# Inverting the chunk matrices of a delta-rule recurrence on TensorE: where the transposed inverse of each level comes from

## What is computed

```
def step(state, inp):
    r_t, w_t, k_t, v_t, kk_t, a_t = inp
    sa = jnp.einsum('bhvk,bhk->bhv', state, kk_t)
    state = (state * w_t[:, :, None, :]
             - sa[..., None] * (kk_t * a_t)[:, :, None, :]
             + v_t[..., None] * k_t[:, :, None, :])
    return state, jnp.einsum('bhvk,bhk->bhv', state, r_t)
```

## Time and profile before

| | |
|---|---|
| median of 3 runs | 3971.02 us (3969.14 to 3973.49) |
| span of the profiled execution | 3972.0 us |
| TensorE busy, of the whole span | 3709.6 us, 93% |
| VectorE busy | 2670.4 us, 67% |
| GpSimd busy | 1955.5 us, 49% |
| the eight tiles' levels and what lies between them | from 515 to 990 us |

### The profile page before, as it was taken

How to read it: one execution, slowest core, us unless ns; L and a number is a source line. 1 busy time by engine, 2 the same in 40 slices (tenths; PEclk the granted TensorE clock), 3 DMA queues, 4 the chain that set the end, 5 groups by cost and what they waited for, 6 DMA issues and landing times.

```text
span 3972.0 us, 55158 instructions
## 1 busy us (share of the span) xinstructions
PE 3709.6 (93%) x19324; PEld 3187.3 (80%) x19324; DVE 2670.4 (67%) x5202; ACT 1244.6 (31%) x1825; POOL 1955.5 (49%) x1352
## 2 busy tenths in 40 slices
PE   8988799999898899999999999999789999899999
PEld 6854488988777678899999998999667888678777
DVE  5443367776322438748887887877797666598887
ACT  3013333332211321233333333323233333333333
POOL 1023122222100016888888888888888888222220
PEclk9989989999999999999999999999889999999999
DMA  3259400000320034478888888887889999899997
GB/s 114 95 192 399 163 19 9 18 18 0 106 90 27 27 106 92 78 199 264 265 270 269 265 261 247 260 263 212 246 210 278 278 282 253 282 384 381 371 380 267
DMA packets 376223, 788.61 MB, mean 199 GB/s; under 512 B 136992, under 2 KB 245536, under 8 KB 342176
## 3 DMA queue, kind: packets, MB, share of 16 engines
q1 hardware_dynamic: 210208, 451.28, 33.7%
q0 software_dynamic: 165888, 336.01, 28.9%
HBM read 643.09 MB, written 144.05 MB: 198 GB/s over the span
## 4 chain that ended last, share of the span: by engine, by line
PE 26%; POOL 15%; DMA 7%; DVE 6%; issue 6%; DVEq 2%; ACT 1%; SPq 1%; POOLq 0%; ACTq 0%
POOL gates_d L2066 12%; PE peer_ps L2176 12%; PE peer_ps L2085 9%; PE peer_ps L2099 4%; DMA peer_gat<-gates_d 3%; DMA late_in<-gates_d 3%; POOL rows L2054 2%; POOL peer_rows L2054 2%; DVE late_rows L2459 1%; DVEq L2389 1%; DVE peer_acc L2474 1%; PE peer_ps L2122 1%; DVEq L2473 1%; DVE late_in L2481 1%; DVE peer_al L2493 0%
## 5 line engine op out<-in xcount | busy, mean ns | idle before, releaser
L2066 POOL DMA_INDIRECT gates_d<-peer_gates,peer_idx x768 | 1366.5, 1779 | 300.9 <-issue 221.2
L2085 PE MATMUL peer_ps<-high,peer_uh 128*128 128x384 f32 x2048 | 528.8, 339 | 38.0 <-DVE peer_ul L2376 32.0
L2085 PE MATMUL peer_ps<-low,peer_uh 128*128 128x384 f32 x2048 | 524.2, 337 | 0.0
L2085 PE MATMUL peer_ps<-high,peer_ul 128*128 128x384 f32 x2048 | 523.6, 336 | 0.0
L2085 PEld LDWEIGHTS peer_ps<-high,peer_uh 128*128 128x128 f32 x2048 | 370.5, 189 | 51.5 <-issue 44.5
L2085 PEld LDWEIGHTS peer_ps<-low,peer_uh 128*128 128x128 f32 x2048 | 373.7, 190 | 0.0
L2085 PEld LDWEIGHTS peer_ps<-high,peer_ul 128*128 128x128 f32 x2048 | 373.3, 189 | 0.0
L2176 PE MATMUL peer_ps<-peer_vh,peer_ah 128*128 128x512 f32 x1026 | 326.8, 400 | 40.3 <-DVE peer_al L2493 40.0
L2054 POOL DMA_INDIRECT late_rows<-in_expert_uv,peer_idx x108 | 139.1, 1288 | 412.1 <-DVE peer_acc L2474 369.6
L2176 PE MATMUL peer_ps<-peer_vh,peer_al 128*128 128x512 f32 x1026 | 322.1, 395 | 0.0
L2176 PE MATMUL peer_ps<-peer_vl,peer_ah 128*128 128x512 f32 x1026 | 321.4, 395 | 0.0
(11 more groups left out here) (480 smaller groups left out, 7697.4 us busy)
## 6 DMA issues: line engine op xcount, KB each, us to landing
late_in<-in_expert_uv SPq DMA_DIRECT2D x170, 512.0 KB
gates_d<-mla_zeros POOLq DMA_DIRECT2D x128, 512.0 KB
hidden_d<-peer_hid SPq DMA_DIRECT2D x128, 384.0 KB
peer_raw<-in_expert_u SPq DMA_DIRECT2D x86, 512.0 KB
peer_val<-in_expert_uv SPq DMA_DIRECT2D x86, 512.0 KB
late_in<-hidden_d SPq DMA_DIRECT2D x170, 192.0 KB
late_in<-gates_d SPq DMA_DIRECT2D x170, 192.0 KB
first_raw<-in_expert_u SPq DMA_DIRECT2D x42, 512.0 KB
```

Of the source, the lines that this page charges most:

```text
L2066: pool.indirect_dma_start(gates_flat, bass.IndirectOffsetOnAxis(ap=idx[:, n, k:k + 1], axis=0), gates[:, n, k:k + 1], None, compute_op=ALU ...
L2085: last = nc.tensor.matmul(ps[i][:, a, 0:HD], w[:, cols], x[:, kc, a * HD:(a + 1) * HD], start=(kc == 0 and w is uh[i % 2] and x is high), ...
```

## The change

At levels 1 to 4 the third product (z transposed) and the masked copy into `yi[e]` go. Instead TensorE transposes the new X itself, `xi[e]`, into `bank[4 + e]`, directly after the next level's P products of that half, and signals a new semaphore `x_turned`. VectorE, after both masked copies into `xi`, waits for it and copies the whole bank into `yi[e]`. The preparing step of the level on VectorE stays behind these copies.

```
@@ TensorE, solve, level l, half e @@
                         inc(last, "p_mm")
+                        if l > 1:
+                            for f in range(PAIRS):
+                                last = nc.tensor.transpose(bank[4 + e][:, f, :], xi[e][:, f, :], consts["ident"][:, :])
+                            inc(last, "x_turned")
...
                         for f in range(PAIRS):
                             last = nc.tensor.matmul(bank[2 + e][:, f, :], yi[e][:, f, :], pe_s[e][:, f, :],
                                                     start=True, stop=True)
-                            if l < 5:
-                                last = nc.tensor.matmul(bank[4 + e][:, f, :], pe_s[e][:, f, :], yi[e][:, f, :],
-                                                        start=True, stop=True)
                         inc(last, "z_mm")
@@ VectorE, solve, level l @@
                         inc(nc.vector.copy_predicated(xi[e][:, :, :], where(level_t, l), bank[2 + e][:, :, :]), "inv")
-                        if l < 5:
-                            inc(nc.vector.copy_predicated(yi[e][:, :, :], where(consts["level"], l),
-                                                          bank[4 + e][:, :, :]), "inv_t")
+                    if l < 5:
+                        for e in range(2):
+                            w.wait("x_turned", 2 * (l - 1) + e + 1)
+                            inc(nc.vector.tensor_copy(flat(yi[e]), flat(bank[4 + e])), "inv_t")
                     if l > 1:
                         prepare_next(l - 1)
```

More of the change, by code:

```diff
@@ L875, in rwkv_stage @@
                         ("ux", 1), ("ux_taken", 1), ("preset", 2), ("copied", 2), ("inv", 12), ("inv_t", 10), ("p_mm", 10), ("p_taken", 10),
-                        ("z_mm", 10), ("u_mm", 2), ("nu", 2), ("at_mm", 2), ("e_mm", 2), ("diag", 2), ("at", 2),
+                        ("z_mm", 10), ("x_turned", 8), ("u_mm", 2), ("nu", 2), ("at_mm", 2), ("e_mm", 2), ("diag", 2), ("at", 2),
                         ("q_mm", 1), ("q1", 1), ("chain", 2), ("state", 2), ("y_mm", 1), ("y", 1), ("mean", 1),
```

## The result

The changed kernel takes 3977.41 us, the median of 20 runs (3967.26 to 4014.81); the kernel before took 3962.26 us beside it (20 runs, 3945.06 to 3979.01). The ratio is 1.0046, 95% interval 1.0031 to 1.0061: slower by about 18 us (the medians themselves lie 15.2 us apart).

What follows compares the result with a forecast made beforehand. TensorE was taken to end levels 2 and 3 of a loop tile, VectorE levels 1 and 4. Queues +12.5 and clock +10.5 gave +23 us on 3972.0, 3995; 1 us less for the median: 3994 us, range 3975 to 4013.

Steps and rivals of the forecast that it cites:

- rival 1: Recurrence: queues cost time but TensorE's pauses pass without a clock fall; +12.5 us, 3983.5 us; chance 0.25.
- The queue on VectorE: Loop tiles: preparing work waits behind `yi` copies; steps 4.77, 8.1 to 8.2, 8.61, 5.37 us; +2.3 us a tile.
- Leaving level 5: End of a tile's levels: second `xi` copy and `kap` come sooner, 1.34 instead of 1.74 us, -0.40 us.
- The prices: Levels 1 to 4: four transposes take 0.44 us, a copy from PSUM into `yi` 0.69 us.
- The dear end of this term: Levels 1 to 4: transposes as slow as products, 0.90 for 0.44 us, add +6.0 us a tile.
- The clock: First seven tiles: TensorE's pauses bring one fall each to 0.50 for 3.4 us, costing 1.5 us; 10.5 us total.
- I leave both as they are: Recurrence: the two clock falls already in the kernel before, one of 10.2 us, were assumed to stay unchanged.
- second rival: Recurrence: today's two long clock falls may go, 9.3 us back, with no new ones; +3 us, 3974 us; chance 0.10.
- The rule of the Trainium skill: Every level: 0.88 us of transposes would be pauses to the clock gate, giving about 4012 us instead of 3994.
- third rival: Recurrence: clock stays low longer, through the narrow products after level 5; 4006 to 4018 us; chance 0.15.
- Rival 4: All levels: TensorE decides, each shortens by its saving of 0.9 us; 29 us faster, 3942 us; chance 0.05.
- Outside the recurrence no instruction changes: Stages outside the recurrence: no instruction changes; their time moving by more than 3 us would show the forecast wrong.

Runs made afterwards that it cites:

- experiment 2: The changed kernel with VectorE's preparing step moved ahead of the copies into `yi`: 3967.8 us, ratio 1.002 to the kernel before.
- Experiment 3: The changed kernel with ScalarE instead of VectorE copying the transposes into `yi`: 3951.8 us, ratio 0.9974 to the kernel before.
- experiment 5: The changed kernel with each transpose done as an ordinary float32 product with the identity: 4010.16 us, one run.
- Experiment 4: The changed kernel with unread products filling TensorE's pauses, 8 after `z` of level 1 and 12 after `z` of level 4: 3982.51 us, ratio 1.005 to the kernel before.
- experiment 9: The changed kernel run again without edits, for a third profile: 3993.94 us, one run.
- experiment 7: The changed kernel with ScalarE copying into `yi`, plus six unread products after `z` of level 1 and two before the narrow products: 3940.53 us, ratio 0.9941 to before.

## Why the prediction was right, and where it was not

The forecast was slower, 3994 us, with a range from 3975 to 4013 us. The 20 runs gave 3977.41 us, close to the lower end. Of the 17 us between, 9 are the starting point: the kernel before took 3962 us beside the change, not the 3971 us of the three runs I had. The ratios of the two timings make the change +18 and +28 us, for a forecast of +23. The time alone doesn't tell the forecast from rival 1 (+12.5 us, no falls); the falls in the traces do.

**The queue on VectorE: right.** The steps were predicted as 4.77, 8.1 to 8.2, 8.61 and 5.37 us and measured as 4.75, 8.12, 8.69 and 5.50. The last two were short by the time from the preparing step to the next beat: 4.33 us from the scan where I took 4.22, 1.13 us from the norms where I took 0.98. Leaving level 5 gained more than thought: the stretch from the last beat to the next tile's first shrank by 0.58 us, not 0.40. The errors cancel, which is luck, and a clean tile grew by 2.30 us as forecast. The last tile's levels took 4.76 us (4.77 forecast). That this order is the cause is shown by experiments 2 and 3, in opposite ways of removing it.

**The prices: right.** The transposes took 0.43 us a group (0.44 taken), the copy from PSUM 0.69 us (0.69 taken). The dear end of this term, transposes as slow as products, was put at +6.0 us a tile beside the kernel before (2.3 and 3.7); experiment 5 has 65.59 us against 59.75, +5.8. Summed over eight tiles, levels at full clock take 453.3 us in the changed kernel (tiles of 62.36, 5 x 62.05 and 61.67 us, last tile 4 x 4.76) and 439.7 us before (60.3 for the first tile, 5 x 59.75, 59.38, last tile 21.2): **+13.6 us.** The forecast of +12.5 counts 0.9 us gained ahead of the first beat, which these lengths don't hold (from the first product to that beat 4.10 us instead of 4.99), so it is +13.4 to compare. The first tile's step from level 3 to 4 was 8.96 us where loop tiles have 8.69, with VectorE idle for 0.65 instead of 0.38 us before the beat ("issue"); why is open.

**The clock: the new falls right, the old ones wrong.** One fall in each of seven tiles at 1.5 us was forecast, 10.5 us. The three profiles had 4, 8 and 8, which cost 459.67 - 453.3 = 6.4, 12.7 and 13.7 us, mean 10.9; 13 came with the 21 pauses before level 5, 7 after the 18 of 2.1 us before level 2. The sum is right and its picture is not: not one fall in each tile, but none in 8 of the 21 tiles, one in 6 and two in 7. I had taken only one of the two pauses of a tile to be followed by a fall, and that one always. One fall of 3.4 us cost 1.3 to 1.7 us. Experiment 4 speaks for the pauses as their cause. The step that failed is "I leave both as they are": the long falls of the kernel before were in none of the three profiles of the change. They had cost 9.8, 9.8 and 3.3 us, mean 7.6. So the levels moved by 13.6 + 10.9 - 7.6 = 16.9 us where the sum says 23. Why the long falls went with the change is open. That the timed +18 and +28 us lie on either side of 23 is no proof of the sum, since the term left out is 7.6 us. My second rival had the long falls go too, but held that no new ones come; half of it was true.

**The rule of the Trainium skill** ("TensorE: Matmul & The Clock Gate", Part 4), by which transposes don't count as busy for the clock gate, pointed at the third rival, 4006 to 4018 us. Experiment 5 speaks against it here: with products in their place the falls were six and longer, not fewer than the 4, 8 and 8 of the change. In experiment 4 every transpose stayed in its place, the pauses alone were filled, and there was no fall. The granted clock over its loop tiles, transposes included, reads 1.00.

**Rival 4,** that TensorE decides: a level did shorten by 0.9 us wherever TensorE ends it, in the last tile (5.67 to 4.76). In the loop tiles VectorE ended it, as argued from the earlier trace rows. Experiment 3 is what that rival described, with a third of its gain (the timing gives 0.26%, 10 us, of its 29).

**"Outside the recurrence no instruction changes"** holds for the program, not for its time: the condition that nothing there moves by more than 3 us was broken in every profile, by the attention stage that runs ahead of the recurrence and that the change can't reach by any wait. One profile of each kernel would have charged it to the change: of the 41 us between the two first spans 12.9 lie ahead of the first beat, 10.2 in the levels and 18.1 behind the last beat. Behind the last beat the three profiles of before have 2999.0, 2987.7 and 2982.0 us and those of the change 3017.1, 2990.6 and 2989.2, so this part differs more within a kernel than between the means of the two. The part ahead of the first beat is 11 to 13 us longer in all three of the change.

## What to carry to other kernels

When an operation gets a new wait, ask first what stands behind it in that engine's queue and who ends the next step; here TensorE won 0.9 us per level, three of the four steps grew by 0.5 to 1.5 us all the same, and the same copy on an engine with slack turned +0.7% into -0.26% (timed side by side). A pause of 2 to 3 us on TensorE can cost more than itself, since the clock may fall for 3.4 us after it. Idle products that fitted into it left the steps unchanged; where there was no pause they were paid for, 1.5 us for 8 and 2.6 us for 12. Compare clean stretches of two traces before comparing spans.

## What the runs showed of the hardware

**Whether a pause makes the clock fall is not fixed.** The same 3.1 us pause before level 5 (3.4 us in the first tile) came with a fall in 13 of 21 cases, the 2.1 us pause before level 2 in 7 of 18, and the 1.8 us pause before level 2 of the last tile in none of 3. In one of the 13, in the first tile of experiment 9, the fall of 6.8 us began 1.1 us before the pause ended. Which tiles have one differs between executions, though the instructions start at the same distances.

**Falls can lock to a loop.** In experiment 2 four tiles in a row took 64.87 us to within 0.01 us, each with its 10.2 us fall 31.0 us after its first beat. The tiles on either side, of the same instructions, took 60.32 and 60.00 us. What selects the state is open. Two products ahead of the narrow ones (experiment 7) went with none of these in two profiles, where the same kernel without them had two long falls and one in two profiles. That these two products did it is not shown: experiment 7 also fills the pause before level 2, and the change and experiment 4 had no long fall without them.

**The attention stage has two lengths,** 217 and 232 us, with the same instructions. The long form has three falls more of the clock, of 3.4, 23.9 and 6.8 us; half of these 34.1 us is 17, for 15 us of difference. The same window inside it in two profiles of experiment 7's kernel, the long form first:

```profile
386.00:409.90 23.90, 22.16 (x48) 10.76 (x49) 6.37 (x21) 4.15 (x11) 0.00 (x0) 0.50 1.03 407
```

```profile
386.00:409.90 23.90, 21.03 (x85) 10.32 (x84) 9.92 (x33) 6.41 (x16) 0.00 (x0) 1.00 1.03 406
```

In 23.9 us the long form got through 48 records of TensorE where the short one did 85, with the same DMA rate. In the six profiles with the long form the stage's first product starts at 258.6 to 259.5 us, in the eight others at 259.7 to 261.4 us; which of the two follows from the other, or both from a third thing, is not shown. What decides it is open. Of the seven timed runs of this kernel the slowest, 3975.07 us beside 3933.90 to 3943.61 us for the other six, is the one whose profile shows the long form. The short form of that kernel was taken on another chip, but these six times on the same one speak for the execution and not the chip.
